# Time mix solved in three parts, one pass for two norms, silus after the next weights, in a one-core kernel of three layers

## The chip, the core and the metric

The kernel runs on one core of one Trainium2 chip. The metric is the device time of one execution in microseconds.

## The reference, cut to what matters

512 tokens of width 1024 pass through a gated layer with its MLP, an RWKV-7 layer ("time mix") with its MLP, a final norm, and a hybrid layer (neighbourhood attention and a bidirectional gated delta net, then a mixture of 64 experts). All in float32. What the change touches:

```python
def step(state, inp):                       # wkv7_scan, per head of 64
    r_t, w_t, k_t, v_t, a_t, b_t = inp
    sa = jnp.einsum('bhvk,bhk->bhv', state, a_t)
    state = (state * w_t[:, :, None, :] + sa[..., None] * b_t[:, :, None, :]
             + v_t[..., None] * k_t[:, :, None, :])
    y_t = jnp.einsum('bhvk,bhk->bhv', state, r_t)
    return state, y_t
...
h = h + conv_ffn(rms_norm(h, norm_ffn_g[i]), ...)
x = rms_norm(h, norm_final_g)               # first norm
h = rms_norm_2(x, ln1_g); proj = h @ w_in   # second norm; x is wanted later as the residual
...
qkv = jax.nn.silu(conv(qkv_raw))            # 5 taps over the sequence, 1536 features
```

## The kernel before, in words

Features lie on partitions, tokens along the free dimension. Every large product is made of three passes over a high and a low part of weights and inputs (lines 590 to 592). A weight item (128 x 2048, two output tiles of 128 features) is loaded by SP, its high part copied by ScalarE (`weight_high`, 550), its low part by VectorE (`weight_low`, 556). `next_high(i)` and `next_low(i)` prepare item i + 1. Two items are held, so the high part of an item waits until TensorE has finished the item two before.

**Order.** Each engine has its own list of instructions, issued in order, with waits on semaphores. Where two stretches of work share an engine they are written as generators and `weave`d: one step of the first, one of the second, in turn, and `nothing(n)` yields n empty steps. The order is therefore fixed by hand, by where the `yield`s stand.

**Time mix.** The scan is done in 8 chunks of 64 tokens for 16 heads, in four quarters q of four heads (two feature tiles). Per quarter, the *solve*: `solve_pe` makes for 8 banks of PSUM (4 to 7, in turn) the products of keys with queries (1439), ScalarE copies one half to MT (1509), VectorE masks the others into ZZ and RKB (1553, 1554); 4 banks of turned keys (1449) go to KBT (1515), 2 banks of products with the values (1464) to AKV (1522). Meanwhile the unit triangular matrices are inverted: SP takes the 16x16 diagonal blocks of MT through DRAM to FB (1307, 1311), VectorE inverts them by 15 block rows (1352, 1355, 1359), SP carries them back into TT and TN by 16 transfers (1316, 1322). POOL clears those first and masks MT into T (1331, 1332, 1409). Then 10 banks of merges on TensorE (1480, 1492), with ScalarE (1531) and VectorE (1577), give the inverse of 64x64 matrices in TT. The *recurrence* of a quarter is a chain of 8 chunks of three steps: products with the state (1603, 1604), VectorE forms RH (1671) and Y1 (1676), TensorE applies TT (1611), ScalarE copies to VU (1655), TensorE forms the new state and output (1622, 1628), VectorE adds and decays the state (1681, 1684, 1686).

The first solve stands alone, with the turning of the values (1253, copied by VectorE, 1289) and the gate (1266, 1267; 1278 on ScalarE) woven in. For q = 0, 1, 2, three steps of solve q + 1 stand ahead of recurrence q, and the rest is woven with it; recurrence 3 is woven with the group norms of the first six tiles. There are two sets of results (TT, RKB, AKV, KBT), used in turn. The residual, set aside in DRAM, comes back to H in one transfer ahead of recurrence 3 (1814); H holds K.B until then.

**Norms.** After the second MLP's down product (`residual_dve`, 708) a column sum of squares and Ln, Exp give the final norm's factor, which VectorE applies to H in place (698). Then eight squares (627, 631), their sum (640), a column sum and Ln, Exp give the second norm's factor; its scaled rows (683) are split into high and low parts (665, 670), and the product in2_qk begins.

**Projection of the delta net.** Eight items; each of the first twelve tiles m is evicted by ScalarE with the middle tap (2050), four taps are added by VectorE (2126) and ScalarE makes the silu and a square (2055, 2058). The next item's weights are made at each even m, ahead of tile m. Sums of the squares of tiles 0 to 7 (1933) stand on TensorE between the sixth and the seventh item.

## Time and profile before

| | us |
|---|---|
| median of 3 runs | 2713.65 (2712.34 to 2713.84) |
| profiled execution, its own time | 2714.64 |
| its span | 2712.9 |
| TensorE busy (matmul) | 2284.6, 84% |
| VectorE busy | 1166.7, 43% |
| ScalarE busy | 858.0, 32% |
| GpSimd busy | 163.3, 6% |
| mean granted TensorE clock | 0.878 |

The span runs from the first to the last instruction. Matmul ends are modelled, so a busy TensorE isn't one at its peak. A clock of 1.00 is 2.4 GHz, one of 0.50 is 1.2 GHz. In the page's forty slices the DMA share stays at 0.9 or more from the thirty-third slice to the thirty-ninth, where the experts' weights are read at about 400 GB/s; ahead of that it is mostly 0.1 to 0.2.

### The profile page before, as it was taken

How to read it: one execution, taken by the hardware profiler on the slowest of the kernel's cores; microseconds unless marked ns; L12 is line 12 of the kernel's file. 1: busy time of each engine (PE TensorE's matmuls, PEld its weight loads, DVE VectorE, ACT ScalarE, POOL GpSimd, SP SyncE). 2: the span in 40 equal slices, each digit the busy share in tenths (PEclk: the TensorE clock that was granted, in tenths of full speed). 3: DMA queues.
4: the chain of work that ended last, by engine and by line, in shares of the span. 5: the costliest groups of instructions: out<-in, count | busy, mean ns of one | idle time of the engine just before them, and what ended most of it. 6: DMA issues, size and time to landing. Idle time of an engine off the chain costs nothing. (4 is left out here: it accounts for less than half of the span.)

```text
span 2712.9 us, 32509 instructions
## 1 busy us (share of the span) xinstructions
PE 2284.6 (84%) x13804; PEld 1676.2 (62%) x13804; DVE 1166.7 (43%) x1846; ACT 858.0 (32%) x1275; POOL 163.3 (6%) x174
## 2 busy tenths in 40 slices
PE   6898999967998776689999888875987688877885
PEld 5777888856766665468888767664975533333332
DVE  4336665356485554456663343645434311111112
ACT  4324443246563222344442244534113110100000
POOL 0000000000002110000000000000410011111110
PEclk9888999988999776789999989876858699999988
DMA  5111322222211001212222223121004399999996
GB/s 191 63 62 62 104 98 85 96 76 87 76 63 17 14 13 40 76 64 96 107 84 96 100 72 108 47 63 22 4 32 191 134 420 418 416 406 406 400 400 253
DMA packets 106597, 377.26 MB, mean 139 GB/s; under 512 B 54960, under 2 KB 55744, under 8 KB 67536
## 3 DMA queue, kind: packets, MB, share of 16 engines
q1 hardware_dynamic: 84848, 296.44, 29.5%
q10 hardware_dynamic: 9216, 67.11, 6.0%
q0 software_dynamic: 12384, 11.58, 1.5%
q8 instruction: 111, 1.82, 0.3%
q14 instruction: 38, 0.31, 0.0%
HBM read 375.31 MB, written 27.53 MB: 148 GB/s over the span
## 5 line engine op out<-in xcount | busy, mean ns | idle before, releaser
L590 PE MATMUL ps<-xh,wh 128*128 128x512 f32 x1384 | 557.9, 403 | 93.0 <-DVE wl L556 44.0
L591 PE MATMUL ps<-xl,wh 128*128 128x512 f32 x1384 | 552.4, 399 | 0.0
L592 PE MATMUL ps<-xh,wl 128*128 128x512 f32 x1384 | 550.7, 398 | 0.0
L556 DVE TENSOR_TENSOR wl<-raw,wh 128x2048 fp32r<-128x2048 f32 (+2 forms) x127 | 264.4, 2082 | 317.8 <-ACT wh L550 317.8
L590 PEld LDWEIGHTS ps<-xh,wh 128*128 128x128 f32 x1384 | 268.0, 194 | 170.6 <-issue 56.2
L3105 PE MATMUL ps<-egu,XT 128*64 128x512 f32 x1088 | 272.0, 657 | 84.5 <-DMA egu<-e_up 80.4
L592 PEld LDWEIGHTS ps<-xh,wl 128*128 128x128 f32 x1384 | 267.8, 193 | 57.9
L591 PEld LDWEIGHTS ps<-xl,wh 128*128 128x128 f32 x1384 | 268.6, 194 | 56.2 <-issue 0.2
L550 ACT ACTIVATE wh<-raw 128x2048 fp32r<-128x2048 f32 (+2 forms) x127 | 220.2, 1734 | 83.2 <-PE ps L875 69.2
L3105 PEld LDWEIGHTS ps<-egu,XT 128*64 128x64 f32 x1088 | 94.2, 151 | 238.9 <-issue 225.4
L3123 DVE TENSOR_TENSOR HIDT<-ps,SIL 128x256 f32<-128x256 f32 x34 | 14.4, 425 | 350.0 <-ACT SIL L3115 350.0
L873 PE MATMUL ps<-HH,wh 128*128 128x512 f32 x352 | 137.2, 390 | 3.1 <-DVE wl L556 3.1
L3115 ACT ACTIVATE SIL<-ps 128x256 f32<-128x256 f32 x34 | 13.1, 385 | 400.5 <-PE ps L3105 400.5
L874 PE MATMUL ps<-HL,wh 128*128 128x512 f32 x352 | 137.0, 389 | 0.0
L875 PE MATMUL ps<-HH,wl 128*128 128x512 f32 x352 | 136.9, 389 | 0.0
L3157 PE MATMUL ps<-ed,HID 128*64 128x512 f32 x544 | 125.6, 604 | 4.1 <-DMA ed<-e_down 3.0
L921 DVE SCALAR_TENSOR_TENSOR tmp<-ps,prm,tmp 128x511 f32<-128x511 f32 x88 | 66.0, 750 | 103.5 <-ACT tmp L897 103.5
L897 ACT ACTIVATE tmp<-ps,prm 128x512 f32<-128x512 f32 x88 | 67.9, 772 | 108.4 <-PE ps L592 108.4
L631 ACT ACTIVATE tmp<-H 128x512 f32<-128x512 f32 x49 | 30.6, 630 | 174.4 <-DVE H L711 170.4
L711 DVE TENSOR_TENSOR H<-ps,H 128x512 f32<-128x512 f32 x40 | 27.5, 689 | 124.6 <-PE ps L875 73.4
L665 ACT ACTIVATE xh<-tmp 128x512 fp32r<-128x512 f32 x94 | 58.4, 626 | 65.4 <-DVE tmp L832 29.6
L3157 PEld LDWEIGHTS ps<-ed,HID 128*64 128x64 f32 x544 | 36.9, 138 | 67.7 <-issue 62.7
(473 smaller groups left out, 3260.8 us busy)
## 6 DMA issues: line engine op xcount, KB each, us to landing
egu<-e_gate SPq DMA_DIRECT2D x68, 1024.0 KB, 14.5
egu<-e_up SPq DMA_DIRECT2D x68, 1024.0 KB, 25.1
ed<-e_down ACTq DMA_DIRECT2D x64, 1024.0 KB, 11.1
raw<-up SPq DMA_DIRECT2D x44, 1024.0 KB, 4.8
raw<-down SPq DMA_DIRECT2D x32, 704.0 KB, 4.0
raw<-rwkv_kr SPq DMA_DIRECT2D x8, 1024.0 KB, 4.8
raw<-in_dn SPq DMA_DIRECT2D x8, 1024.0 KB, 4.9
raw<-sgu_u SPq DMA_DIRECT2D x4, 1024.0 KB, 8.3
```

The source lines that it names most:

```text
L550: e.activation(K.WH[s][:, 0:n], K.RAW[r][:, 0:n], ACT.Copy).then_inc(*K.w_high.mark(i))
L556: e.tensor_tensor(K.WL[s][:, 0:n], K.RAW[r][:, 0:n], K.WH[s][:, 0:n].bitcast(F32), SUB).then_inc(*K.w_low.mark(i))
L590: e.matmul(o, h[:, q, k], x_high[:, k], start=k == 0, stop=False)
L591: e.matmul(o, h[:, q, k], x_low[:, k], start=False, stop=False)
L592: last = e.matmul(o, l[:, q, k], x_high[:, k], start=False, stop=k == KT - 1)
L873: e.matmul(o, h[:, c], HH[:, k], start=k == 0, stop=False)
L874: e.matmul(o, h[:, c], HL[:, k], start=False, stop=False)
L875: last = e.matmul(o, lo[:, c], HH[:, k], start=False, stop=k == FT - 1)
L897: e.activation(z, K.ps[:, u % 8], ACT.Identity, bias=K.prm("cb", 44 * l + f), scale=K.prm("cw", (3 * l + 2) * 44 + f)).then_inc(*K.act_out ...
L921: e.scalar_tensor_tensor(z[:, 1:S], o[:, 0:S - 1], K.prm("cw", (3 * l + 1) * 44 + f), z[:, 1:S], MUL, ADD).then_inc(*K.conv.mark(up, m, 0))
L3105: last = e.matmul(K.ps[rows, b].rearrange("p (a n) -> p a n", a=2), K.XT[:, b, k, rows], K.EGU[(2 * q + z) % 5][:, :, k], start=k == 0, st ...
L3157: last = e.matmul(K.ps[rows, 4 + 2 * b + c], K.HID2[:, b, j, rows], K.ED[(2 * q + z) % 4][:, j, 512 * c:512 * c + 512], start=j == 0, stop ...
```

## The change

The solve becomes three parts. `front_*(q)` is everything up to AKV, `rows_dve(q)` the block rows, `back_*(q)` the merges. Fronts 0 and 1 and back 0 stand ahead of recurrence 0; recurrence q then carries front q + 2 with rows q + 1 in its first half (12 steps, one bank per step for the first eight), and back q + 1 in its second half (12 steps). There are three sets of TT, RKB and AKV, two of MT, and the turned keys are written over the keys and K.B themselves. The values are turned inside front 0 and copied by ScalarE; the gate is woven with front 1. H comes back in two transfers, the second (tiles 6 and 7) behind the first output weights.

For the two norms, each residual tile's square is added twice, once plain and once weighted by the final gain squared plus eps, so that the second norm's factor follows at once from 1/sqrt(mean + eps^2). The rows for in2_qk are scaled by the product of both gains; the final norm of H comes later, after the low part of in2_qk's second item.

In the projection, ScalarE evicts both tiles of an item, makes the weights of the item after next, and then the silus and squares; VectorE makes the low part between the second tile's taps and its norm. Cut to its core:

```diff
+        shapes = dict(TT=[128, 16, 64], RKB=[128, 16, 2, 64], AKV=[128, 4, 256])
         self.sets = []
-        for q, x in enumerate((cut0, q0)):
-            one = {}
-            one["TT"], one["RKB"], one["AKV"], one["KBT"], _ = self.lay(
-                x, (f"qTT{q}", [128, 16, 64]), (f"qRKB{q}", [128, 16, 2, 64]), (f"qAKV{q}", [128, 4, 256]),
-                (f"qKBT{q}", [128, 4, 2, 256]))
-            self.sets.append(one)
+        for i, at in enumerate((dict(TT=q0, RKB=q0 + 4096, AKV=q0 + 12288), dict(TT=cut0, RKB=cut0 + 4096, AKV=cut0 + 12288),
+                                dict(TT=cut0 + 16384, RKB=ring0 + 8192, AKV=cut0 + 20480))):
+            self.sets.append({x: self.lay(at[x], (f"q{x}{i}", shapes[x]))[0] for x in shapes})
         self.TN, self.ZZ, x = self.lay(cut0 + 24576, ("TN", [128, 16, 64]), ("ZZ", [128, 16, 64]))
         assert x <= cut0 + 32768
-        self.MT, self.ST, self.RH, self.VU, self.Y1, x = self.lay(
-            ring0, ("MT", [128, 16, 64]), ("ST", [128, 2, 64]), ("RH", [128, 2, 2, 64]), ("VU", [128, 2, 2, 2, 64]),
-            ("Y1", [128, 2, 64]))
+        self.MT = [self.lay(x, (f"MT{i}", [128, 16, 64]))[0] for i, x in enumerate((ring0, q0 + 16384))]
+        self.ST, self.RH, self.VU, self.Y1, x = self.lay(
+            ring0 + 4096, ("ST", [128, 2, 64]), ("RH", [128, 2, 2, 64]), ("VU", [128, 2, 2, 2, 64]), ("Y1", [128, 2, 64]))
...
+def last_residual_dve(K, e, m):
+    u = K.u["down1"] + m
+    e.wait_ge(*K.gemm_sum("down1", m))
+    e.tensor_tensor(K.H[:, m], K.ps[:, u % 8], K.H[:, m], ADD).then_inc(*K.dve_out.mark("down1", m))
+    K.board.empty(u, K.dve_out("down1", m))
+    e.wait_ge(*K.square("n_fin", m))
+    x = K.T[1 + m % 3]
+    if m == 0:
+        e.wait_ge(*K.normed("weights"))
+        e.tensor_scalar(K.T[0], x, K.FW[:, 0:1], None, MUL).then_inc(*K.sumsq.mark("n_ln1", 0))
+        e.tensor_copy(K.T[4], x).then_inc(*K.sumsq.mark("n_fin", 0))
+        return
+    e.wait_ge(*K.sumsq("n_ln1", m - 1))
+    e.scalar_tensor_tensor(K.T[0], x, K.FW[:, m:m + 1], K.T[0], MUL, ADD).then_inc(*K.sumsq.mark("n_ln1", m))
+    e.wait_ge(*K.sumsq("n_fin", m - 1))
+    e.tensor_tensor(K.T[4], K.T[4], x, ADD).then_inc(*K.sumsq.mark("n_fin", m))
...
+def last_norms_act(K, e):
+    e.wait_ge(*K.normed("eps"))
+    rows_rstd_act(K, e, "n_ln1", K.T[5], K.EE[:, 0:1])
+    for k in range(KT):
+        x_high_act(K, e, "in2_qk", k, K.T[1 + k % 3], K.normed("n_ln1", k), K.XH)
+    rows_rstd_act(K, e, "n_fin", K.T[4], K.prm("eps"))
...
+def turned_keys(K, q, c):
+
+    return (K.B if c else K.KB)[:, 2 * q:2 * q + 2].rearrange("p a (b k) -> p (a b) k", k=256)
...
+def front_act(K, e, q):
+    s, MT, AKV = f"f{q}", K.MT[q % 2], set_of(K, q)["AKV"]
...
+    for hl in range(4):
+        it = slice(4 * hl, 4 * hl + 4)
+        for c in range(2):
+            v = 2 * hl + c
+            across = slice(64 - 64 * c, 128 - 64 * c)
+            o = K.ps[:, solve_bank(s, v)].rearrange("p (n a j) -> p n a j", n=4, a=2)
+            e.wait_ge(*K.solve_sum(q, v))
+            e.activation(MT[across, it], o[across, :, 0], ACT.Copy).then_inc(*K.act_solve.mark(q, "m", v))
+            yield
...
+    e.wait_ge(*K.solve_sum(q, "kbt", 1, 1))
+    for c in range(2):
+        for jl in range(2):
+            v = 8 + 2 * c + jl
+            e.activation(turned_keys(K, q, c)[:, :, 128 * jl:128 * jl + 128], K.ps[:, solve_bank(s, v)].rearrange("p (n k) -> p n k", n=4),
+                         ACT.Copy).then_inc(*K.act_solve.mark(q, "kbt", c, jl))
...
+def front_dve(K, e, q):
+    s, RKB = f"f{q}", set_of(K, q)["RKB"]
+    if q == 0:
+        e.wait_ge(*K.turn_sum("vt", 7))
+        e.wait_ge(*K.dve_scale(KT - 1, "bv"))
+    for hl in range(4):
+        it = slice(4 * hl, 4 * hl + 4)
+        for c in range(2):
+            v = 2 * hl + c
+            own = slice(64 * c, 64 * c + 64)
+            o = K.ps[:, solve_bank(s, v)].rearrange("p (n a j) -> p n a j", n=4, a=2)
+            e.wait_ge(*K.act_solve(q, "m", v))
+            e.tensor_tensor(K.ZZ[own, it], o[own, :, 0], K.mask("stru", 4)[own], MUL).then_inc(*K.dve_solve.mark(q, "zz", v))
+            e.tensor_tensor(RKB[:, it, c], o[:, :, 1], K.mask("incu", 4), MUL).then_inc(*K.dve_solve.mark(q, "rkb", v))
+            K.board.empty(("solve", SOLVE_AT[s] + v), K.dve_solve(q, "rkb", v))
+            yield
+    yield from nothing(4)
...
+def rows_dve(K, e, q):
...
+        if n % 2 == 0:
+            yield
+    e.wait_ge(*K.dve_diag(name, 15, "sum"))
+    e.tensor_copy(X[:, 1], X[:, 0].rearrange("p i j -> p j i")).then_inc(*K.dve_diag.mark(name, "both"))
+    yield from nothing(5)
...
 def rwkv_pe(K, e):
     project_pe(K, e)
-    weave([solve_pe(K, e, 0), gate_and_values_pe(K, e)], 2)
+    first = front_pe(K, e, 0)
+    for _ in range(4):
+        next(first)
+    values_pe(K, e)
+    weave([first], 1)
+    weave([front_pe(K, e, 1), gate_pe(K, e)], 2)
+    weave([back_pe(K, e, 0)], 1)
     for q in range(3):
-        ahead = solve_pe(K, e, q + 1)
-        for _ in range(3):
-            next(ahead)
-        weave([recur_pe(K, e, q), ahead], 2)
-    K.board.point("PE", "reload")
+        weave([recur_pe(K, e, q), chain(front_pe(K, e, q + 2) if q < 2 else nothing(12), back_pe(K, e, q + 1))], 2)
     weave([recur_pe(K, e, 3), chain(*(group_pe(K, e, js) for js in EARLY_GROUPS))], 2)
...
 def rwkv_dve(K, e):
     project_dve(K, e)
-    weave([solve_dve(K, e, 0), values_dve(K, e)], 2)
+    weave([front_dve(K, e, 0)], 1)
+    second = front_dve(K, e, 1)
+    for _ in range(6):
+        next(second)
+    weave([second, rows_dve(K, e, 0)], 2)
+    weave([back_dve(K, e, 0)], 1)
     for q in range(3):
-        ahead = solve_dve(K, e, q + 1)
-        for _ in range(3):
-            next(ahead)
-        weave([recur_dve(K, e, q), ahead], 2)
+        beside = abreast(front_dve(K, e, q + 2) if q < 2 else nothing(12), rows_dve(K, e, q + 1))
+        weave([recur_dve(K, e, q), chain(beside, back_dve(K, e, q + 1))], 2)
     weave([recur_dve(K, e, 3), chain(*(group_dve(K, e, js) for js in EARLY_GROUPS))], 2)
...
 def rwkv_sp(K, e):
     project_sp(K, e)
     for q in range(4):
-        for _ in solve_sp(K, e, q):
-            pass
+        solve_sp(K, e, q)
     e.wait_ge(*K.h_out("hs"))
-    e.wait_ge(*K.board.at("PE", "reload"))
-    e.dma_start(K.H[:, :, :], K.hs).then_inc(*K.h_in.landing("hs"))
+    e.wait_ge(*K.recur_sum(2, 7, "s"))
+    e.dma_start(K.H[:, 0:6], K.hs[:, 0:6]).then_inc(*K.h_in.landing("most"))
     for t in K.board.all_at("rwkv"):
         e.wait_ge(*t)
-    load_weights(K, e, K.first["rwkv_o"], K.first["up1"])
+    load_weights(K, e, K.first["rwkv_o"], K.first["rwkv_o"] + 1)
+    e.dma_start(K.H[:, 6:8], K.hs[:, 6:8]).then_inc(*K.h_in.landing("hs"))
+    load_weights(K, e, K.first["rwkv_o"] + 1, K.first["up1"])
...
-    norm_in_place_dve(K, e, "n_fin", "fing", 0)
-    for k in range(KT):
-        sumsq_dve(K, e, "n_ln1", k)
-    norm_dve(K, e, "n_ln1", "ln1", 0, "in2_qk")
-    for i in range(4):
+    last_norms_dve(K, e)
+    next_low(K, e, K.first["in2_qk"])
+    last_norm_in_place_dve(K, e)
+    for i in range(1, 4):
         next_low(K, e, K.first["in2_qk"] + i)
...
+    next_high(K, e, K.first["in2_dn"])
+    for i in range(6):
+        middle_tap(2 * i)
+        middle_tap(2 * i + 1)
+        next_high(K, e, K.first["in2_dn"] + i + 1)
+        features(2 * i)
+        features(2 * i + 1)
...
         K.board.empty(u, K.conv("in2_dn", m, 3))
+        if m % 2:
+            next_low(K, e, K.first["in2_dn"] + m // 2 + 1)
```

`back_pe`, `back_act` and `back_dve` hold the merges as before, with a step for each bank and `nothing(2)` or `nothing(4)` to keep the steps level. `solve_sp` and `solve_pool` lose their steps: SP and POOL run through each quarter in order, behind semaphores alone; POOL clears TN and TT for quarter q after the last merge of q - 1.

## Rows read from the trace of the kernel before

**Rows 1.** Order of time, TensorE, start of the time mix: start us, us, engine line op.
```profile
810.03 0.32 PE L1439 MATMUL ps<-AR,KB 64*64 64x128 f32 x1
...
816.69 0.32 PE L1449 MATMUL ps<-cst,KB 128*64 128x128 f32 x1
...
818.59 1.09 PE L1253 MATMUL ps<-cst,VF 128*128 128x128 f32 x8
...
828.23 1.12 PE L1266 MATMUL ps<-HID,raw 128*128 128x512 f32 x2
...
830.34 1.12 PE L1266 MATMUL ps<-HID,raw 128*128 128x512 f32 x2
...
846.35 2.08 PE L1480 MATMUL ps<-TN,tmp 64*64 64x64 f32 x64 [1.20 <-DMA TN<-rw0xd]
```

**Rows 2.** Order of time, VectorE, start of the time mix.
```profile
812.38 0.42 DVE L1553 TENSOR_TENSOR ZZ<-ps,cst 64x256 f32<-64x256 f32 x1 [0.67 <-ACT MT L1509]
...
825.48 0.15 DVE L1352 TENSOR_TENSOR rw0PR<-rw0FB,rw0X 128x1 f32<-128x1 f32 x1
...
834.56 0.38 DVE L1359 COPY rw0X<-rw0X 128x256 f32<-128x256 f32 x1
...
856.70 0.69 DVE L1577 TENSOR_TENSOR qTT<-ps,qTT 128x512 f32<-128x512 f32 x1 [0.24 <-PE ps L1492]
...
863.30 0.17 DVE L1666 MEMSET ST<- 128x128 f32 x1 [0.17 <-DVE qRKB L1554]
```

**Rows 3.** Order of time, VectorE: the state cleared ahead of recurrences 1 to 3.
```profile
928.11 0.17 DVE L1666 MEMSET ST<- 128x128 f32 x1 [0.16 <-DVE qRKB L1554]
...
991.47 0.17 DVE L1666 MEMSET ST<- 128x128 f32 x1 [0.16 <-DVE qRKB L1554]
...
1052.38 0.17 DVE L1666 MEMSET ST<- 128x128 f32 x1 [0.16 <-DVE qTT L1577]
```

**Rows 4.** Order of time, VectorE, chunks 5 to 7 of the first recurrence.
```profile
895.76 0.42 DVE L1671 TENSOR_TENSOR RH<-ps,qAKV 64x256 f32<-64x256 f32 x1 [0.80 <-PE ps L1604]
...
900.88 0.43 DVE L1671 TENSOR_TENSOR RH<-ps,qAKV 64x256 f32<-64x256 f32 x1 [1.03 <-PE ps L1604]
...
912.00 0.29 DVE L1681 TENSOR_TENSOR ST<-ST,ps 128x128 f32<-128x128 f32 x1 [10.05 <-PE ps L1628]
```

**Rows 5.** Busy time by window: us, PE, PEld, DVE, ACT, POOL, PEclk, DMA share, GB/s.
```profile
884.00:888.00 4.00, 2.65 (x36) 2.21 (x33) 3.63 (x13) 0.38 (x1) 0.00 (x0) 0.50 0.02 4
```

**Rows 6.** Order of time, VectorE, ScalarE and TensorE, the two norms after the last MLP.
```profile
1556.71 5.39 DVE L698 SCALAR_TENSOR_TENSOR H<-H,prm,tmp 128x512 f32<-128x512 f32 x8 [3.88 <-ACT tmp L658]
...
1570.34 1.28 ACT L658 ACT_TABLE_LOAD   x1
...
1572.30 1.41 DVE L683 SCALAR_TENSOR_TENSOR tmp<-H,prm,tmp 128x512 f32<-128x512 f32 x2 [4.83 <-ACT tmp L658]
...
1574.54 0.77 PE L590 MATMUL ps<-xh,wh 128*128 128x512 f32 x1 [4.94 <-issue]
...
1581.99 1.90 ACT L550 ACTIVATE wh<-raw 128x2048 fp32r<-128x2048 f32 x1
...
1583.93 2.29 DVE L556 TENSOR_TENSOR wl<-raw,wh 128x2048 fp32r<-128x2048 f32 x1 [1.11 <-ACT wh L550]
```

**Rows 7.** Order of time, VectorE and TensorE, projections of the second layer.
```profile
1601.93 2.29 DVE L556 TENSOR_TENSOR wl<-raw,wh 128x2048 fp32r<-128x2048 f32 x1 [8.59 <-ACT wh L550]
...
1612.81 2.29 DVE L556 TENSOR_TENSOR wl<-raw,wh 128x2048 fp32r<-128x2048 f32 x1 [8.59 <-ACT wh L550]
...
1660.17 0.80 PE L590 MATMUL ps<-xh,wh 128*128 128x512 f32 x1 [4.72 <-DVE wl L556]
...
1730.32 3.10 DVE L2126 SCALAR_TENSOR_TENSOR tmp<-ps,prm,tmp 128x510 f32<-128x510 f32 x4
...
1741.48 3.59 PE L1933 MATMUL ps<-AT,cst 128*128 128x512 f32 x8
...
1754.82 0.77 PE L590 MATMUL ps<-xh,wh 128*128 128x512 f32 x1 [3.64 <-DVE wl L556]
```

More of the change, by code:

```diff
@@ L719, in sgu_sp, with last_norm_in_place_dve @@
+def last_norm_in_place_dve(K, e):
+    e.wait_ge(*K.rstd("n_fin", "r"))
+    for k in range(KT):
+        e.scalar_tensor_tensor(K.H[:, k], K.H[:, k], K.prm("fing", k), K.T[4], MUL, MUL).then_inc(*K.normed.mark("n_fin", k))
 def sgu_sp(K, e):
@@ L906, in ffn_act @@
             next_high(K, e, K.first[down] + 2 * m + part)
-        residual_act(K, e, down, norm, m)
+        if l:
+            last_square_act(K, e, m)
+        else:
+            residual_act(K, e, down, norm, m)
     K.board.point("ACT", "ffn", l)
@@ L934, in ffn_dve @@
             next_low(K, e, K.first[down] + 2 * m + part)
-        residual_dve(K, e, down, norm, m)
+        if l:
+            last_residual_dve(K, e, m)
+        else:
+            residual_dve(K, e, down, norm, m)
     K.board.point("DVE", "ffn", l)
@@ L1242, in low_emptied, with values_pe @@
     return K.board.emptied(("low", i - 4) if i >= 4 else last_use(K, i))
-def gate_and_values_pe(K, e):
-    yield from nothing(4)
+def values_pe(K, e):
+    e.wait_ge(*K.act_out("turn5", KT - 1))
     for i in range(8):
@@ L1254, in gate_and_values_pe, with values_act, gate_pe @@
         last.then_inc(*K.turn_sum.mark("vt", i))
-        if i % 4 == 3:
-            yield
-    yield from nothing(2)
+def values_act(K, e):
+    for i in range(8):
+        n, half = i // 2, i % 2
+        e.wait_ge(*K.turn_sum("vt", i))
+        e.activation(K.VT[:, n, 512 * half:512 * half + 512], K.ps[:, i % 4], ACT.Copy).then_inc(*K.act_out.mark("vt", i))
+        K.board.empty(("low", i), K.act_out("vt", i))
+def gate_pe(K, e):
     item = K.first["lora2b"]
@@ L1279, in gate_act @@
         K.board.empty(("low", 8 + m), K.act_out("lora_g", m))
-        if m % 2:
-            yield
-def values_dve(K, e):
-    yield from nothing(4)
-    for i in range(8):
-        n, half = i // 2, i % 2
-        e.wait_ge(*K.turn_sum("vt", i))
-        e.tensor_copy(K.VT[:, n, 512 * half:512 * half + 512], K.ps[:, i % 4]).then_inc(*K.dve_out.mark("vt", i))
-        K.board.empty(("low", i), K.dve_out("vt", i))
-        if i % 4 == 3:
-            yield
+        yield
 SPOTS = [(r, slice(64 * (r // 4) + 16 * (r % 4), 64 * (r // 4) + 16 * (r % 4) + 16), slice(16 * (r % 4), 16 * (r % 4) + 16))
@@ L1391, in solve_pool @@
-def solve_pool(K, e, q):
-    K.board.point("POOL", "solve", q)
-    z = K.sets[q % 2]
-    for _ in range(4):
-        yield
-    bl = diagonal_pool(K, e, f"rw{q}", K.TN, z["TT"], 0, before_solve(K, q) + [K.solve_sum(q, 7)])
-    next(bl)
-    for _ in range(3):
-        yield
-    for _ in bl:
-        yield
-        yield
+SOLVE_AT = {}
+for stage, n in (("f0", 14), ("f1", 14), ("b0", 10), ("f2", 14), ("b1", 10), ("f3", 14), ("b2", 10), ("b3", 10)):
+    SOLVE_AT[stage] = SOLVE_AT["end"] if SOLVE_AT else 0
+    SOLVE_AT["end"] = SOLVE_AT[stage] + n
@@ L1410, in solve_pool, with front_pe @@
                 [128, 8, 64]), MUL).then_inc(*K.pool_solve.mark(q, "masked", i, l))
-        yield
-    for _ in range(6):
-        yield
-def solve_pe(K, e, q):
-    K.board.point("PE", "solve", q)
-    z = K.sets[q % 2]
+def front_pe(K, e, q):
     for j in (2 * q, 2 * q + 1):
-        e.wait_ge(*K.dve_scale(j, "r"))
         e.wait_ge(*K.dve_scale(j, "k inv"))
@@ L1425, in take @@
         nonlocal v
[L1426 removed]
+        for t in solve_emptied(K, f"f{q}", v):
             e.wait_ge(*t)
         v += 1
[L1429 removed]
+        return solve_bank(f"f{q}", v - 1)
     for hl in range(4):
@@ L1469, in solve_pe, with back_pe, take @@
+def back_pe(K, e, q):
+    TT = set_of(K, q)["TT"]
+    v = 0
+    def take():
+        nonlocal v
+        for t in solve_emptied(K, f"b{q}", v):
+            e.wait_ge(*t)
+        v += 1
+        return solve_bank(f"b{q}", v - 1)
     e.wait_ge(*K.inv_in[f"rw{q}"](f"rw{q}", 7, 1))
@@ L1581, in solve_dve, with abreast @@
+            yield
+    yield from nothing(2)
+def abreast(*stretches):
+    left = list(stretches)
+    while left:
+        for g in list(left):
+            try:
+                next(g)
+            except StopIteration:
+                left.remove(g)
+        if left:
             yield
 def recur_pe(K, e, q):
-    z = K.sets[q % 2]
+    z = set_of(K, q)
     K.board.point("PE", "recur", q)
@@ L1709, in group_emptied @@
     if g < 4:
-        return K.board.emptied(("solve", 3, 20 + g))
+        return K.board.emptied(("solve", SOLVE_AT["end"] - 4 + g))
     first, i = EARLY_GROUPS[(g - 4) // 6], (g - 4) % 6
@@ L1850, in rwkv_act @@
     project_act(K, e)
-    weave([solve_act(K, e, 0), gate_act(K, e)], 2)
+    first = front_act(K, e, 0)
+    for _ in range(4):
+        next(first)
+    values_act(K, e)
+    weave([first], 1)
+    weave([front_act(K, e, 1), gate_act(K, e)], 2)
+    weave([back_act(K, e, 0)], 1)
     for q in range(3):
-        ahead = solve_act(K, e, q + 1)
-        for _ in range(3):
-            next(ahead)
-        weave([recur_act(K, e, q), ahead], 2)
+        weave([recur_act(K, e, q), chain(front_act(K, e, q + 2) if q < 2 else nothing(12), back_act(K, e, q + 1))], 2)
     weave([recur_act(K, e, 3), chain(*(group_act(K, e, js) for js in EARLY_GROUPS))], 2)
```

296 lines of the change are left out of this document (163 added, 133 removed).

## The prediction

> **What bounds the kernel now.** I read the page of the profile first: TensorE is the busiest engine almost everywhere, and only the expert part at the end is held by DMA. The change touches neither the expert part nor the gated MLPs' inner loops. It touches three stages ahead of them, which hand on to what follows by data, so what they gain or lose should reach the end in full. In each I looked for the wait that ends last.
>
> In the time mix (810 to 1106 us) I went by the order of time on TensorE and VectorE. The solve of the first quarter stands alone. TensorE does the first solve sums, the keys turned and the values turned, then the gate from 828.23 [rows 1]. VectorE works on the 16x16 blocks from 825.48 to 834.94 [rows 2], the inverse travels by DMA, and TensorE's merge sums begin at 846.35 [rows 1], 11.4 us after the blocks. They end at 857.4 (856.70 plus 0.69), and the first recurrence starts at 863.30 [rows 2]. The four recurrences start at 863.30, 928.11, 991.47 and 1052.38 [rows 2, 3]: 64.8, 63.4 and 60.9 us apart. A chunk with little beside it takes 5.1 us (895.76 to 900.88). The chunk in which the next inverse is awaited takes 14 more, with 10.05 us of idle VectorE [rows 4]. Where the recurrence runs nearly alone, TensorE's granted clock is 0.50, which is 1.2 GHz [rows 5].
>
> At the two norms VectorE makes the final norm at 1556.71, the inner norm's scaled rows at 1572.30, and TensorE starts its product at 1574.54 [rows 6]. In the delta net's projection, TensorE waits for low halves of weights that VectorE writes late: six items run from 1660.17 to 1741.48, 81.3 us, where an item without waits takes 10.88 (1601.93 to 1612.81), and the sums of squares after them hold the seventh item until 1754.82 [rows 7].
>
> **Start of the time mix: a loss.** I counted each queue's new order. TensorE does the same work as before up to the gate (four banks of the first front, values, four banks, turned keys, values' products), so the second front and the gate can start at 828.2 as the gate does now [rows 1]. The matrix of the first quarter is complete some 5 us later than now, because eight banks of values (1.09 us for two) now stand inside it. That costs nothing by itself: something later holds the blocks. VectorE must do six banks of the **second** front before the first quarter's blocks, then the seventh, two block rows, the eighth, and only then the rest. On TensorE each of those banks alternates with one gate sum of 2.11 us (828.23 to 830.34), and a bank takes 0.83 (810.03 to 816.69 for eight). So the eighth bank is done at 828.2 + 7 x 2.94 + 0.83 = 849.6; its copy and masks make 850.9. The rest of the blocks, 8.7 of their 9.5 us, ends at 859.6, where it ends at 834.9 now. Then 11.4 us of DMA, to 871.0, and the merge, 11 us at the full clock. TensorE has run out of work at about 857 (gate, keys and products done), so I take 3 us more for a merge that starts at 1.2 GHz. The first recurrence starts at 885 in place of 863.3: **+21.7**. Bounds: +18 (full clock; the four second-front banks that now precede 863.30 are inside this already) and +25.
>
> **The three periods: a gain.** Chunks 0 to 2 of a recurrence now carry eight front banks and all block rows. VectorE is the tight queue: eight banks of two 0.42 us operations [rows 2] (6.3 us as spaced), 9.5 us of blocks, and 1.7 us per chunk of its own, 20.4 us for 2.7 chunks that take 13.7 alone. I wrote down step by step what each queue has ahead of the recurrence's next operation (a bank's sums on TensorE, its copy on ScalarE, two masks and two block rows on VectorE), and three chunks come to 21.9 us at 2.4 GHz and 27.6 at 1.2. Chunk 3 carries four banks of turned keys, their four ScalarE copies in one go ahead of the recurrence's own, and two banks of products: 7 to 11.4. The front half is 29 to 39 us. The inverse arrives 11.4 us after the blocks end, at 33 to 37, so at the full clock a stall of 4 us closes much of that span; I take 34. The back half has ten merge banks of 1.04 us (2.08 for 64 passes, two banks) [rows 1], and a bank nearly fits the gap at each step: 20 at full clock, 26 with a slow start, 22 taken. Periods of **56** for the first two, bounded by 53 and 65. The third has no front: blocks beside bare chunks end at 14.7, the inverse comes at 26, then 23 us: **49**, with 46 and 53 as ends. Against 64.8, 63.4 and 60.9 that is -8.8, -7.4 and -11.9, together **-28.1**. The fourth recurrence and its groups are left as they are. The set of results that is third, and the keys that are turned into their own place, only allow this order; they add no operation. The 0.5 MB of residual now loaded after the first output weights is wanted ten microseconds later, and I cost it at nothing; without that cover it is about 2 us. Net time mix: 21.7 - 28.1 = **-6.4**.
>
> **One pass for two norms.** Out of the path go eight in-place products, eight squares with sums, one column sum and one Ln-Exp pair. The first scaled row can be written when the in-place norm starts now: 1572.30 - 1556.71 = 15.6 us [rows 6]. The two extra VectorE operations per residual tile hide under the 15 us that TensorE spends on each. But the second Ln-Exp pair, for the final norm, now stands on ScalarE between the last high half of x and the second weight item's high half (1581.99 now). Ln, Exp of 0.7 and 0.6 and two table loads of 1.28 make 3.9 us, while the low half of that item ends now at 1586.2 (1583.93 plus 2.29), about when TensorE wants it [rows 6]. So 3.4 us come back as a stall: **-12.2**. Ends: -15.6 and -9. The in-place norm then sits behind that item's low half and is over before the next. The rows show the operation after a table load starting 1.29 us after it, without further cost. The Trainium skill, "ScalarE: Activation LUTs", section "What ACT_TABLE_LOAD costs", puts a drain of about 1380 ns on top of each; by that the stall would be 6.1 us and this part -9.5. I go by the rows.
>
> **Silus later.** Now ScalarE makes the next weights only after the silu, so VectorE's low half ends some 12 us after the item. In the new order VectorE needs tap 0.8, two convolutions of 3.10, one norm of 0.7 and a low half of 2.3, 9.8 us in all, before the next but one item can be used, and TensorE takes 10.88: it fits with 1 us to spare. The third item's sigmoid and exponentials (four table loads) slip it by about 0.5 and the first item starts slowly, so 65.3 + 1.6 in place of 81.3: -14.4. The squares then wait only for the last convolution, 8.9 us where 13.3 pass now, without the late weights: -4.4. The first wait, 4.72 us, stays: its item is prepared where it was. **-18.8**, ends -12 and -20.
>
> **Sum.** -6.4 - 12.2 - 18.8 = -37.4. The profiled execution took 2714.64 (span 2712.9), 1.0 above the median of the runs, so I carry the difference over: 2713.65 - 37.4 = 2676.
>
> **Rivals.**
> (a) The recurrence hides its company better: TensorE at 2.4 GHz throughout, periods of 53, 53 and 46, and a start of +18. That is 13 us more: 2663. For it: merge and front banks packed densely did run at 1.00. Against: VectorE's 20.4 us don't depend on that clock. If besides the blocks of the first quarter were not held by the gate, another 15 us would go: 2650. Together 0.2.
> (b) TensorE falls back to 1.2 GHz in both front halves: periods of 65, 65 and 53, start +25. The time mix is then 19 slower and the whole 2702. For it: 884 to 888 stands at 0.50 with TensorE two thirds busy [rows 5]. 0.15. The Trainium skill, "TensorE: Matmul & The Clock Gate", section "A second HAM failure mode: psum-queue depth-cycling", describes short idles between groups of matmuls that make the clock swing; that rule is on this side.
> (c) VectorE's 1 us of slack in the projection isn't there, and waits return at every item: 10 us back, 2686. 0.1.
> (d) Slower than before. TensorE is at 1.2 GHz already when gate and second front alternate (828 to 858). Each round takes 5.9, the eighth bank ends at 871, the first recurrence starts at 915 (+52), and periods of 70, 70 and 56 add 7: +59 against -31 elsewhere, 2742. It decides from the point where the time mix loses more than 31. Against it: the gate's sums run at the full clock now. 0.04.
> (e) The new order of the projection does nothing because weights arrive late by DMA (4.9 us each against 13 available): 2695. 0.03.
>
> **Numbers.** Forecast 2676 with 0.48. The range 2654 to 2702 takes in (a) mostly, (b) and (c). A difference of 0.2% (5.4 us) is about what a measurement of this kernel can tell. Every case but (d) is faster; the upper tails of (b) and (e), which I put at 0.05, reach past 2708 and are split between the same and slower: faster 0.91, same 0.04, slower 0.05. Outside the range lie (d), the best of (a) and those tails, some 0.15.
>
> **What would show it.** In the new profile: the first quarter's blocks ending near 860 and the first recurrence at 880 to 890; TensorE idle for 10 us or more before the first merge; periods near 56, 56 and 49 with no 10 us wait of VectorE in the first two; the in2 product starting 15.6 us after the final norm's Exp moved forward, with one wait of about 3 us at its second item; no wait for low halves after the first of the projection. It is wrong if the first recurrence starts before 870, if periods stay above 62, or if waits for low halves recur.

## The result, and the profile after

| | before | after |
|---|---|---|
| median, us | 2713.36 (2712.34 to 2713.84, 4 runs) | 2678.40 (2677.47 to 2680.04, 4 runs) |
| ratio, 95% interval | | 0.9871 (0.9859 to 0.9884) |
| profiled execution, its span | 2714.64, 2712.9 | 2680.04, 2678.2 |
| mean granted clock | 0.878 | 0.880 |

35.0 us faster; 37.4 were predicted. Of the executions behind the numbers further on, one took 2833.4 us at a mean granted clock of 0.778 and is left out of its median, and two, 2664.9 and 2685.1 at 0.892 and 0.891, lie 29 and 26 us under the median of their fellows (0.875 to 0.881) and are kept. The page after, its span and its busy times:

```profile
span 2678.2 us, 32481 instructions
...
PE 2289.2 (85%) x13804; PEld 1677.3 (63%) x13804; DVE 1163.7 (43%) x1844; ACT 855.7 (32%) x1275; POOL 163.3 (6%) x174
```

TensorE does no less than before. It waits less. Where the 34.7 us of the two spans lie, point by point:

| stretch | before | after | difference | predicted |
|---|---|---|---|---|
| up to the first solve sum | 810.03 | 808.75 | -1.3 | 0 |
| from there to the first recurrence | 53.3 | 76.2 | +22.9 | +21.7 |
| three periods | 189.1 | 161.4 | -27.6 | -28.1 |
| fourth recurrence to the last residual of the MLP | 498.4 | 499.7 | +1.3 | 0 |
| from there to the first item of the projection | 109.4 | 98.4 | -11.0 | -12.2 |
| six items and sums of squares | 94.7 | 77.0 | -17.7 | -18.8 |
| the rest | | | -1.3 | 0 |

(The last residual is 1550.75 before, 1546.05 after; the other points stand in the rows.) The first line is no part of the change: nothing ahead of 810 was edited.

VectorE at the start of the time mix after, in order of time, against [rows 2, 3]:

```profile
828.26 0.42 DVE L1632 TENSOR_TENSOR ZZ<-ps,cst 64x256 f32<-64x256 f32 x1 [6.27 <-ACT MT L1598]
831.38 0.43 DVE L1632 TENSOR_TENSOR ZZ<-ps,cst 64x256 f32<-64x256 f32 x1 [2.38 <-ACT MT L1598]
...
850.15 0.43 DVE L1632 TENSOR_TENSOR ZZ<-ps,cst 64x256 f32<-64x256 f32 x1 [1.74 <-ACT MT L1598]
859.31 0.37 DVE L1658 COPY rw0X<-rw0X 128x256 f32<-128x256 f32 x1
877.75 0.69 DVE L1727 TENSOR_TENSOR TN<-ps,TN 128x512 f32<-128x512 f32 x1 [18.07 <-PE ps L1696]
...
884.96 0.17 DVE L1829 MEMSET ST<- 128x128 f32 x1 [0.16 <-DVE qTT L1727]
...
940.69 0.17 DVE L1829 MEMSET ST<- 128x128 f32 x1 [0.16 <-DVE AR L1849]
...
997.59 0.17 DVE L1829 MEMSET ST<- 128x128 f32 x1 [0.16 <-DVE AR L1849]
...
1046.40 0.17 DVE L1829 MEMSET ST<- 128x128 f32 x1 [0.16 <-DVE AR L1849]
```

The banks of the second front come 3.13 us apart, each behind a gate sum, VectorE idles 2.3 us ahead of each, and the first quarter's blocks, which VectorE does mostly after them, end at 859.7. The periods are 55.7, 56.9 and 48.8. TensorE has nothing to do for 12 us and then starts the merge:

```profile
826.71 0.32 PE L1553 MATMUL ps<-AR,KB 64*64 64x128 f32 x1
...
856.15 2.69 PE L1578 MATMUL ps<-VT,ZZ 64*64 64x64 f32 x64 [0.70 <-ACT KB L1605]
...
871.09 1.22 PE L1684 MATMUL ps<-TN,tmp 64*64 64x64 f32 x17 [12.25 <-DMA TN<-rw0xd]
```

The windows of the three periods, each cut where the merge's first matmul starts (us, busy time of PE, PEld, DVE, ACT, POOL, then the granted clock, the DMA share and GB/s):

```profile
884.96:921.00 36.04, 29.56 (x432) 26.51 (x432) 23.43 (x75) 9.90 (x24) 7.10 (x7) 0.72 0.11 17
921.00:940.69 19.69, 17.76 (x464) 16.94 (x464) 9.80 (x27) 4.78 (x11) 1.64 (x2) 0.91 0.10 15
940.69:976.90 36.21, 31.47 (x432) 28.28 (x432) 23.02 (x75) 9.91 (x24) 5.51 (x6) 0.66 0.11 17
976.90:997.59 20.69, 18.77 (x464) 17.85 (x464) 9.82 (x28) 4.78 (x11) 1.66 (x2) 0.86 0.10 15
997.59:1026.40 28.81, 14.06 (x176) 11.76 (x176) 18.38 (x59) 3.95 (x10) 5.08 (x5) 0.54 0.12 20
```

So one of the first two periods is 36 us up to the merge and 20 behind it, where 34 and 22 were predicted, and the third is 28.8 and 20.0, where 26 and 23 were. What comes before the merge falls in two parts. The next quarter's blocks end 24.0 us after the start of each of the first two recurrences (17.4 in the third). Up to there the windows are:

```profile
884.96:908.96 24.00, 20.31 (x266) 18.31 (x268) 20.06 (x64) 6.07 (x16) 6.70 (x6) 0.62 0.01 2
940.69:964.67 23.98, 22.70 (x266) 20.40 (x268) 19.63 (x64) 6.08 (x16) 5.11 (x5) 0.52 0.01 2
```

Then the inverse travels for 12.1 us (12.3 and 11.4 in the other two), and TensorE, out of work, waits for it: 2.57, 3.22 and 4.45 us ahead of the three merges. The first of them:

```profile
921.05 1.73 PE L1684 MATMUL ps<-TN,tmp 64*64 64x64 f32 x32 [2.57 <-DMA TN<-rw1xd]
```

What VectorE waits for in the fifth chunk of each of the three:

```profile
925.84 0.29 DVE L1844 TENSOR_TENSOR ST<-ST,ps 128x128 f32<-128x128 f32 x1 [6.26 <-PE ps L1791]
...
982.61 0.29 DVE L1844 TENSOR_TENSOR ST<-ST,ps 128x128 f32<-128x128 f32 x1 [7.79 <-PE ps L1791]
...
1031.55 0.29 DVE L1844 TENSOR_TENSOR ST<-ST,ps 128x128 f32<-128x128 f32 x1 [8.47 <-PE ps L1791]
```

At the norms [rows 6], ScalarE, VectorE and TensorE in order of time:

```profile
1549.51 1.28 ACT L756 ACT_TABLE_LOAD   x1 [2.11 <-PE ps L768]
1550.80 0.69 ACT L756 ACTIVATE tmp<-ps,EE 128x512 f32<-128x512 f32 x1
...
1555.78 0.77 PE L589 MATMUL ps<-xh,wh 128*128 128x512 f32 x1 [4.77 <-issue]
...
1562.69 0.63 ACT L664 ACTIVATE xh<-tmp 128x512 fp32r<-128x512 f32 x1 [0.63 <-DVE tmp L783]
1563.34 1.28 ACT L756 ACT_TABLE_LOAD   x1
1564.64 0.69 ACT L756 ACTIVATE tmp<-ps,prm 128x512 f32<-128x512 f32 x1
...
1567.18 1.90 ACT L549 ACTIVATE wh<-raw 128x2048 fp32r<-128x2048 f32 x1
...
1571.45 0.50 PE L589 MATMUL ps<-xh,wh 128*128 128x512 f32 x1 [2.69 <-DVE wl L555]
```

The product starts 9.7 us after the last residual (23.8 before) and waits 2.69 at its second item. In the projection [rows 7] the first item still waits, no later one waits for a low half, and the seventh has a small wait that is new:

```profile
1644.47 0.50 PE L589 MATMUL ps<-xh,wh 128*128 128x512 f32 x1 [4.72 <-DVE wl L555]
...
1712.05 1.45 PE L2099 MATMUL ps<-AT,cst 128*128 128x512 f32 x3
...
1721.43 0.47 PE L589 MATMUL ps<-xh,wh 128*128 128x512 f32 x1 [1.83 <-ACT AT L2162]
```

### The profile page after: what moved, and what is told of

The parts are those of the page before. It is cut to its first block and busy times, and to the rows that moved or that the text cites. A ratio compares the mean times of both kernels' runs of the same rounds, so it can differ in the third digit from the quotient of the medians.

```text
span 2678.2 us, 32481 instructions
## 1 busy us (share of the span) xinstructions
PE 2289.2 (85%) x13804; PEld 1677.3 (63%) x13804; DVE 1163.7 (43%) x1844; ACT 855.7 (32%) x1275; POOL 163.3 (6%) x174
## 5 line engine op out<-in xcount | busy, mean ns | idle before, releaser
L591 PEld LDWEIGHTS ps<-xh,wl 128*128 128x128 f32 x1384 | 265.4, 192 | 57.2
L590 PEld LDWEIGHTS ps<-xl,wh 128*128 128x128 f32 x1384 | 266.0, 192 | 55.7 <-issue 0.7
L3290 DVE TENSOR_TENSOR HIDT<-ps,SIL 128x256 f32<-128x256 f32 x34 | 14.4, 424 | 348.6 <-ACT SIL L3282 348.6
L3324 PEld LDWEIGHTS ps<-ed,HID 128*64 128x64 f32 x544 | 37.4, 139 | 69.9 <-issue 64.0
L958 PEld LDWEIGHTS ps<-HH,wh 128*128 128x128 f32 x352 | 66.1, 188 | 17.7 <-DVE wl L555 4.0
L960 PEld LDWEIGHTS ps<-HH,wl 128*128 128x128 f32 x352 | 66.1, 188 | 13.8
```

The source lines that it names most:

```text
L590: e.matmul(o, h[:, q, k], x_low[:, k], start=False, stop=False)
L591: last = e.matmul(o, l[:, q, k], x_high[:, k], start=False, stop=k == KT - 1)
L958: e.matmul(o, h[:, c], HH[:, k], start=k == 0, stop=False)
L960: last = e.matmul(o, lo[:, c], HH[:, k], start=False, stop=k == FT - 1)
L3324: last = e.matmul(K.ps[rows, 4 + 2 * b + c], K.HID2[:, b, j, rows], K.ED[(2 * q + z) % 4][:, j, 512 * c:512 * c + 512], start=j == 0, stop ...
```

## The experiments

Twelve kernels ran, in four sets; each set has its own runs of the kernel before, whose medians were 2712.8, 2713.5, 2715.4 and 2714.3.

### Each part alone

The kernel before with one of the three parts of the diff and nothing of the others.

> The kernel before with the norms alone changed. If the three parts of the change add up, the prediction's step gives 2713.4 - 12.2 = 2701, with one stall of TensorE of about 3 us at the second item of the in2 product; the trace of the changed kernel, read stage by stage, says -11.4, 2702. Rival (the saved time is waited for again by weights that now come too late): 2706 or more.

2701.9 (three executions), ratio 0.9961 (0.9945 to 0.9977), about where the prediction's step has it. The trace has the same stage as the changed kernel: from the last residual to the product 9.7 us, then a wait of 2.65.

> The kernel before with the projection's silus alone moved. Prediction's step: 2713.4 - 18.8 = 2694.6, no wait of TensorE for a low half after the projection's first item. By the trace of the changed kernel, -17.7: 2695.7. Rival (without the earlier arrival from the norms the loaded weights are late): waits for DMA in the first items and 2700 or more.

2692.6, ratio 0.9903 (0.9856 to 0.9950). The ratio lies lower than the medians' 0.993, since the execution at 2664.9 is in it. First item at 1663.75, squares at 1731.34, seventh item at 1740.70: 67.6 and 9.4 us, the changed kernel's to a tenth. No weight is late, so the rival falls.

> The kernel before with the time mix alone changed. Prediction's step: 2713.4 - 6.4 = 2707, made of a start 21.7 later and periods 28.1 shorter. By what the changed kernel's time leaves when norms and silus are taken off (35.0 - 11.4 - 17.7): -5.9, 2707.5. Rival: the time mix gives nothing by itself (2713) and the other parts were worth more than their stages show.

2710.1, ratio 0.9968 (0.9926 to 1.0009). That interval can't tell -3 from nothing. The trace can: periods of 55.9, 56.8 and 49.0, the first recurrence at 884.66. The parts add up within what these medians can tell: they are 10.9, 20.2 and 2.7 under the runs of before, 33.8 together, where the whole change gave 35.0.

### The first quarter's blocks ahead of the second front

On the changed kernel:

```diff
-    second = front_dve(K, e, 1)
-    for _ in range(6):
-        next(second)
-    weave([second, rows_dve(K, e, 0)], 2)
+    weave([rows_dve(K, e, 0)], 1)
+    weave([front_dve(K, e, 1)], 1)
```

> The changed kernel, but VectorE solves the first quarter's blocks before any bank of the second front. Theory (the blocks were held by the banks that wait for the gate on TensorE, and TensorE then ran dry): blocks end near 838, the inverse is there at 850, the merge begins when TensorE is through with the second quarter's products, near 857, at the full clock, and the first recurrence starts at 867 to 870 in place of 885: 2661 to 2664. Rival 1 (TensorE is held instead, because the four banks of the second front are emptied late): merge from 865, first recurrence near 878, 2672. Rival 2 (TensorE needs the time anyway, the 12 us of idle time only move): 2678.

2663.3, ratio 0.9812 (0.9798 to 0.9826): 15.1 less than the changed kernel. Its VectorE in order of time:

```profile
830.30 0.16 DVE L1651 TENSOR_TENSOR rw0PR<-rw0FB,rw0X 128x1 f32<-128x1 f32 x1 [6.83 <-DMA rw0FB<-rw0md]
...
839.41 0.37 DVE L1658 COPY rw0X<-rw0X 128x256 f32<-128x256 f32 x1
...
863.92 0.69 DVE L1727 TENSOR_TENSOR TN<-ps,TN 128x512 f32<-128x512 f32 x1 [11.41 <-PE ps L1696]
...
871.13 0.17 DVE L1829 MEMSET ST<- 128x128 f32 x1 [0.17 <-DVE qTT L1727]
```

In this execution all is 1.5 later upstream (the second front's first sums are at 828.19). The blocks end 20 us earlier, TensorE goes from the second quarter's products straight into the merge at 859.9, and the merge takes 11.2 us at a clock of 1.00. In the changed kernel it took 13.9, from 871.09 to 884.96, and began at 0.50. So of the 22.9 us that the start lost, 15 are the order on VectorE: 12.3 of idle TensorE and 2.7 of the clock behind it. The expected mechanism is shown, and neither rival. The periods are 57.0, 57.2 and 49.0 here, 1.7 longer in sum than in the changed kernel; why wasn't tried.

### The inverse sooner, in two ways

Block rows beside a recurrence four at a time:

```diff
-        if n % 2 == 0:
+        if n % 4 == 0:
             yield
...
-    yield from nothing(5)
+    yield from nothing(9)
```

> The changed kernel, but the block rows that run beside a recurrence are given out four at a time in place of two, so that they end after half as many steps. Theory (the fifth chunk of each of the first three recurrences waits for the inverse; those waits of VectorE are 6.26, 7.79 and 8.47 us, where a chunk without that wait has about 2.5): blocks end 4 to 6 us earlier in each period, the waits shrink to about 2.5, and 12 to 14 us go: 2665. Rival (VectorE's queue sets the front half, so the time comes back in chunks 0 to 3): 2676 to 2680. Rival 2 (front banks are late and hold TensorE's turned keys): slower, 2682.

2672.1, ratio 0.9842 (0.9826 to 0.9859): 6.3 less. The edit also changes the rhythm of the first quarter's rows, and the first recurrence comes 2.0 sooner after the first sum of the second front. The waits of the fifth chunks are under 2.5 us in the first two recurrences and 4.30 in the third, and yet the periods fell by 1.3, 2.8 and 1.2 alone (54.4, 54.1, 47.6), 5.3 where 12 to 14 were expected. The merge still begins 36.1 and 35.8 us into the first two periods: TensorE has the front's sums and keys ahead of it. What went is in the back half (18.3 where 19.7 and 20.7 stood), and in the third period, where the merge begins after 27.3 in place of 28.8. The theory had the wait right and its worth wrong.

Half of the inverse's transfers on GpSimd's queue:

```diff
 def solve_sp
-        for z, dst in enumerate((TT, K.TN)):
-            ...
+        e.dma_start(K.TN[p, 0:16, c], src).then_inc(*K.inv_in[name].landing(name, r, 1))
 def solve_pool
+    for r, p, c in SPOTS:
+        ...
+        e.dma_start(TT[p, 0:16, c], src).then_inc(*K.inv_pool.landing(q, r))
```

> The changed kernel, but of the 16 transfers of each inverse 8 go out on GpSimd's queue beside 8 on SP's, where all 16 take 7.9 us on SP's now. Theory (the inverse is awaited at the start and in every period): 3.9 us less four times, 2663. If it is awaited only at the start and the waits of the fifth chunks have another cause: 2674. Rival (GpSimd's queue is slower at issuing or landing than SP's): the start of the first recurrence stays at 885 or comes later, 2678 or more.

2669.5, ratio 0.9833 (0.9817 to 0.9850): 8.9 less. From the start of the blocks' last copy to the first merge 9.6 us pass in place of 11.8, and the periods are 54.7, 52.6 and 46.3. The blocks end at 24.0 as before, and the merge follows 11.1 and 10.5 us later in the first two periods. The two queues side by side, SP's and GpSimd's (start, us, eight transfers each):

```profile
863.25 3.76 SPq L1503 DMA_DIRECT2D TN<-rw0xd  x8
```
```profile
863.89 4.73 POOL L1535 DMA_DIRECT2D qTT<-rw0xd  x8 [35.23 <-DMA rw0xd<-rw0X]
```

GpSimd's needs 4.7 us for eight and starts 0.6 later, so 2.2 us are won at the start, not 3.9. The inverse was awaited in all four places, and in the periods it still is: the fifth chunks wait 5.44, 3.39 and 5.97 us.

### The final norm's pair later

```diff
 def last_norms_act
-    rows_rstd_act(K, e, "n_fin", K.T[4], K.prm("eps"))
 def layer2_act
             next_high(K, e, K.first["in2_qk"] + m // 2)
+        if m == 0:
+            rows_rstd_act(K, e, "n_fin", K.T[4], K.prm("eps"))
 def layer2_dve
     next_low(K, e, K.first["in2_qk"])
+    next_low(K, e, K.first["in2_qk"] + 1)
     last_norm_in_place_dve(K, e)
```

> The changed kernel, but ScalarE makes the in2 product's second weight item before the Ln-Exp pair of the final norm, and VectorE writes that item's low half before it normalizes in place. Theory (the pair is what holds TensorE 2.69 us at the second item): that wait goes, 2675.7. Rival (the in-place norm now delays the third item's low half, and the wait returns there): 2678.

2676.0, ratio 0.9856 (0.9838 to 0.9874): 2.4 less, where the wait was 2.69. The interval overlaps that of the changed kernel, so the times alone don't show this gain; the trace shows the wait gone. TensorE has no wait at the second or third item. ScalarE in order of time:

```profile
1565.86 1.90 ACT L549 ACTIVATE wh<-raw 128x2048 fp32r<-128x2048 f32 x1
1567.78 1.28 ACT L756 ACT_TABLE_LOAD   x1
1569.07 0.69 ACT L756 ACTIVATE tmp<-ps,prm 128x512 f32<-128x512 f32 x1
```

### Three of them together, and two variants

> The changed kernel with three of these edits together: the first quarter's blocks ahead of the second front, block rows four at a time, the final norm's pair later. If they add up: 2678.4 - 15.1 - 13 - 2.7 = 2648. If the rows' rhythm gives nothing: 2661.

2653.0, ratio 0.9773 (0.9756 to 0.9789). The single gains as measured, 15.1, 6.3 and 2.4, give 2654.6: they add up. The 2648 expected took 13 for the rows. This is faster than both kernels.

> The three edits together and besides the inverse's transfers on two queues. In the kernel with the three edits no wait for the inverse is left in the fifth chunks, and at the start TensorE has work until the inverse is there; so if those two readings are right, the second queue gives nothing any more: 2651 to 2655. If its gain (8.9 us on the changed kernel) has another source and adds up: 2644.

2653.3, ratio 0.9773 (0.9757 to 0.9790), periods 54.2, 54.0 and 47.4 against 54.2, 54.0 and 47.5. Where nothing waits for the inverse, a faster inverse is worth nothing.

> The changed kernel with the first quarter's blocks ahead of the second front, the final norm's pair later and the inverse's transfers on two queues, but the block rows two at a time as in the changed kernel. With the transfers on two queues alone the periods were 54.7, 52.6 and 46.3 (153.6), with rows four at a time 54.4, 54.1 and 47.6 (156.1). If both cure the same wait and the first does it the cheaper way: 2.5 us under the three edits, 2650.5. If, as with the first quarter's blocks moved, the front loses a rhythm (57.0, 57.2 and 49.0 were measured there): 2654 or more.

2654.1, ratio 0.9771 (0.9754 to 0.9787), periods 54.0, 54.4 and 46.8. Its four executions, 2648.8 to 2655.9, can't tell 2650.5 from 2654. The periods can: their sum is 155.2, against 155.8 with rows four at a time, so no gain of 2.5. Why these periods are 1.6 longer in sum than with the queues alone wasn't tried.

### What sets the front half of a period

Two kernels on top of the three edits. One adds 24 matmuls that nobody reads:

```diff
+def keep_busy(K, e, q, ch):
+    if q < 3 and ch < 4:
+        e.matmul(K.ps[:, 2, 256:512], K.cst("ones", 128), K.cst("eye16", 256), start=True, stop=True)
 def recur_pe
         last.then_inc(*K.recur_sum.mark(q, ch, "a"))
+        keep_busy(K, e, q, ch)
...
         last.then_inc(*K.recur_sum.mark(q, ch, "s"))
+        keep_busy(K, e, q, ch)
```

> The three edits together and 24 matmuls (f32, 128x256) more, whose result nobody reads: two in each of the first four chunks of the first three recurrences, in TensorE's gaps. Question: what sets the front half of a period, 35 us in which the granted clock is 0.61 to 0.71? Theory A (TensorE's clock: the fillers keep it at 2.4 GHz, each costs 0.5 us, and the bank sums and chunk sums halve): 3 to 5 us less in each of the two periods with a front, 2643 to 2648. Theory B (the clock stays at 1.2 GHz, or VectorE's queue sets the pace and the fillers stand in the way): 10 to 20 us more, 2663 to 2673. If VectorE alone sets it and the fillers fit the gaps: 2653.

The other takes VectorE's work away:

```diff
-    for n in range(1, 16):
+    for n in range(1, 16 if q == 0 else 8):
...
+    for _ in range(0 if q == 0 else 2):
+        yield
```

> The three edits together, and the last eight of the fifteen block rows left out for the second to fourth quarter (their results are then incomplete): 6.1 us of VectorE less in each of three periods, the steps in which they are given out as before. Theory A (TensorE at 1.2 GHz sets the front half): 0 to 2 us per period, 2647 to 2653. Theory B (VectorE's queue sets it): 5 to 6 us per period, 2635 to 2638. In the third period, which has no front, VectorE's rows delay the recurrence's own steps either way, so 4 to 6 us go there in both.

2667.9, ratio 0.9825 (0.9808 to 0.9841), and 2633.9, ratio 0.9699 (0.9683 to 0.9715). Windows of the three front halves, from a recurrence's start to the merge's first matmul: of the three edits, of the one with the matmuls, of the one without the rows.

```profile
869.75:905.70 35.95, 28.76 (x430) 26.09 (x431) 23.49 (x72) 9.01 (x22) 7.11 (x7) 0.72 0.15 22
...
923.96:959.70 35.74, 31.80 (x430) 28.82 (x431) 22.08 (x72) 8.90 (x22) 5.50 (x6) 0.62 0.16 24
...
977.96:1005.20 27.24, 14.40 (x176) 12.15 (x176) 17.41 (x56) 3.95 (x10) 5.09 (x5) 0.53 0.13 21
```
```profile
871.10:912.10 41.00, 35.59 (x444) 29.23 (x445) 22.93 (x72) 8.90 (x22) 7.11 (x7) 0.71 0.14 21
...
930.39:972.00 41.61, 37.04 (x446) 30.53 (x447) 22.10 (x72) 8.90 (x22) 5.50 (x6) 0.71 0.13 20
...
990.24:1018.80 28.56, 22.72 (x188) 15.69 (x189) 17.39 (x56) 3.96 (x10) 5.09 (x5) 0.52 0.12 19
```
```profile
868.49:903.00 34.51, 28.78 (x428) 26.58 (x429) 18.28 (x56) 8.89 (x22) 7.10 (x7) 0.70 0.16 25
...
921.30:954.70 33.40, 30.21 (x429) 27.64 (x430) 17.47 (x56) 8.91 (x22) 5.50 (x6) 0.64 0.17 26
...
972.97:996.80 23.83, 13.61 (x174) 11.44 (x175) 12.05 (x40) 3.95 (x10) 5.08 (x5) 0.54 0.16 24
```

The eight added matmuls of a half stand in the trace as two records each, and they keep TensorE busy for 7.7 us in each half with a front and 9.8 in the third. The halves with a front grow by 5.1 and 5.9. TensorE's idle time in them was 7.2 and 3.9 us and is 5.4 and 4.6, so little of the added work found a gap. In the third, which has no front, the idle time fell from 12.8 to 5.8 and the half grew by 1.3. The 2667.9 lies in the range of theory B, which held two causes; the windows speak for TensorE's line of work. The clock rose in one half only (0.62 to 0.71), so what the half would take at 2.4 GHz is still open. Taking 5.2 and 4.6 us of busy time from VectorE shortened those halves by 1.4 and 2.3 only, near theory A's 0 to 2, and the third by 3.4.

That holds for the kernel with the three edits, whose rows are given out sooner. Its first half, cut where the blocks end:

```profile
869.75:888.27 18.52, 11.60 (x166) 10.24 (x168) 16.32 (x50) 3.85 (x10) 6.71 (x6) 0.70 0.01 2
888.27:905.70 17.43, 17.16 (x268) 15.85 (x265) 7.18 (x23) 5.17 (x12) 0.40 (x1) 0.73 0.31 43
```

Up to the blocks' end VectorE is the busy one, and TensorE waits once 5.7 us for it; behind it TensorE is busy 17.2 of 17.4 us, and the inverse is there before its turn comes. In the changed kernel the blocks end at 24.0, the inverse comes last and TensorE waits. So these two experiments don't say what set the halves that the prediction was about.

By its total alone the second kernel would have said the opposite: 19.1 us less, as if VectorE set everything. But the periods account for 6.8 of it. The kernel without the rows computes other values in the time mix, the tokens go to other experts, and one expert's weights fewer are read. The pages' DMA issues, with the three edits and without the rows:

```profile
egu<-e_gate SPq DMA_DIRECT2D x68, 1024.0 KB, 15.3
```
```profile
egu<-e_gate SPq DMA_DIRECT2D x66, 1024.0 KB, 14.5
```

From the first convolution of the projection to the end, 1020.0 and 1006.5 us pass. Nearly all of the difference, 13.2 us, lies between the first and the last product of the experts (529.4 and 516.2).

## Why the prediction was right, step by step

**Start, +21.7; it was +22.9.** The mechanism is the one predicted, and every point of the chain came where the count of the queues put it: eighth bank's masks done at 851.0 (850.9), blocks 859.7 (859.6), first recurrence 884.96 (885), merge 11.2 at the full clock (11) and 2.7 for the slow start (3). That the points agree to 0.1 is partly luck: the second front began at 826.7, 1.5 earlier than the 828.2 counted with, and its banks came 3.13 apart in place of 2.94, which gave 1.3 of that back. Rival (a)'s remark that blocks not held by the gate would give another 15 was worth 15.1.

**Periods, -28.1; they were -27.6,** and the mechanism held: VectorE's queue sets the blocks' end, and the merge waits for the inverse behind it. The 20.4 us of VectorE's work that the text has for 2.7 chunks were 20.1 and 19.6 busy in the 24.0 us up to the blocks' end. That this doesn't depend on the clock is borne out: the blocks end 24.0 us into both periods, at a granted clock of 0.62 and 0.52, and in the kernel with the first quarter's blocks moved at 24.0 too, with 0.68 in its second period. (No run took work from VectorE in this order of the rows, so this rests on the traces alone.) The inverse's arrival at 36.1 and 36.2 lies in the 33 to 37 of the text. What was off are two sizes, and that they cancel is luck. The front half was 36.0 and 36.2, where 34 was taken from near the lower end of that span. The back half was 19.7 and 20.7 where 22 was: it ran at 0.91 and 0.86, near the full clock, for which the text has 20. In the third period it is the same: 28.8 for 26, its blocks ending at 17.4 in place of 14.7, and 20.0 for 23. (One reading of the trace before is unclear: the chunk that awaits the inverse there takes 14.7 us in all, from 900.88 to 915.55, which is 9.6 more than one that doesn't; no sum uses it.)

**Rival (b), 0.15:** its condition came, its price didn't. TensorE was at 1.2 GHz in most of both front halves: its granted clock was 0.50 from 895 to 910, with TensorE busy 14.6 of the 15 us. The Trainium skill, "TensorE: Matmul & The Clock Gate", section "A second HAM failure mode: psum-queue depth-cycling", describes such a swing between the two clocks, and the windows agree with the swing (0.78, 0.50 and 0.95 in the stretches of the first half that 895 and 910 part); the short idles that it names as the cause are not shown here. Periods of 65 were priced, a front half of 39 and a back half of 26, where 36 and 20 came. The 27.6 us written for three chunks at 1.2 GHz was near: VectorE's first operation of the fourth chunk comes 26.7 after the start of the first recurrence (911.70). But chunk 3 up to the merge took 9.3 where the slow clock was to make it 11.4, and the back half was not slow.

**The wait for the inverse** was given as 4 us. TensorE waits 2.6, 3.2 and 4.5 for it ahead of the merge; VectorE waits 6.3 to 8.5 in the fifth chunks, of which about 2.5 stand in a chunk without that wait. Shortening it gave 6.3 (rows, 2.0 of it at the start) or 8.9 (queues) in all. A wait's length on the trace is not its worth, because other work stood behind it in line: with the rows given out sooner the merge began no earlier in the first two periods.

**Norms, -12.2; they were -11.0.** The stall was 2.69 where 3.4 stood. The product starts 14.1 earlier relative to the last residual, not 15.6: ScalarE now loads Ln's table only after the column sum (1549.51), 1.28 us in the open. The operation after a load starts 1.29 us after the load's start again (1549.51 to 1550.80, 1563.34 to 1564.64). The Trainium skill, "ScalarE: Activation LUTs", section "What ACT_TABLE_LOAD costs", adds a drain of about 1380 ns to a load; by the estimate worked out from it the stall would have been 6.1. No drain shows in this trace, and the rows decided rightly. These sizes make -11.4; where the other 0.4 went wasn't looked for.

**Silus, -18.8; they were -17.7.** Six items 67.6 us in place of 81.3 (-13.7, predicted -14.4), squares and sums 9.4 in place of 13.3 (-4.0, predicted -4.4). The 1 us of slack held at every item. (Its terms, 0.8, twice 3.10, 0.7 and 2.3, make 10.0 and not 9.8, so it was 0.9.) The difference is partly the 1.83 us at the seventh item, whose bank ScalarE's Ln empties late; it was not in the text. Rivals (c) and (e) didn't come.

**At nothing:** the second transfer of the residual cost nothing (from VectorE's last addition to the state to the last residual 445.4 before, 445.1 after). The fourth recurrence, left as it was, took 54.5 in place of 53.0. The windows of both, before and after:

```profile
1052.38:1060.00 7.62, 6.76 (x51) 3.84 (x52) 4.03 (x10) 3.89 (x8) 0.00 (x0) 1.00 0.80 280
```
```profile
1046.40:1054.00 7.60, 6.74 (x47) 3.67 (x48) 3.44 (x8) 2.15 (x5) 0.00 (x0) 0.78 0.59 209
```

The clock is lower at its start now. That this costs the 1.5 us wasn't tried.

By the spans the sum was 2.7 us too good: 1.2 at the start, 0.5 in the periods, 1.3 behind them, 1.2 and 1.1 in the other two parts, less the 1.3 ahead of the time mix and the 1.3 at the end that belong to no part.
